# The token halves of a sorted expert stage: copied in a row, and gathered with weights eight columns apart

## The reference, cut to what matters

```python
    g_logits = (t @ w_rg).astype(F32) + b_rg.astype(F32)
    ...
    top_v, top_i = lax.top_k(e_sel, TOP_K_IN_GROUP)
    ...
    hg = jnp.einsum('td,edf->tef', t, w_gate)
    hu = jnp.einsum('td,edf->tef', t, w_up)
    act = jax.nn.silu(hg) * hu * combine[..., None].astype(t.dtype)
    return jnp.einsum('tef,efd->td', act, w_down).reshape(b, L, d)
```

## Time and profile before

| | |
|---|---|
| median of 3 runs | 938.12 us (934.38 to 943.42) |
| the profiled execution | 942.36 us, span 940.6 us |
| mean granted TensorE clock | 0.959 of full speed |
| busy: TensorE products / weight loads | 864.2 us / 521.8 us |
| busy: VectorE / ScalarE / GpSimd | 407.9 / 219.3 / 131.4 us |
| moved by DMA | 190.38 MB |

### The profile page before, as it was taken

How to read it: one execution, slowest core, us unless ns; L and a number is a source line. 1 busy time by engine, 2 the same in 40 slices (tenths; PEclk the granted TensorE clock), 3 DMA queues, 4 the chain that set the end, 5 groups by cost and what they waited for, 6 DMA issues and landing times.

```text
span 940.6 us, 12273 instructions
## 1 busy us (share of the span) xinstructions
PE 864.2 (92%) x4528; PEld 521.8 (55%) x4528; DVE 407.9 (43%) x975; ACT 219.3 (23%) x432; POOL 131.4 (14%) x243
## 2 busy tenths in 40 slices
PE   6699999999789969999989999789999999999795
PEld 3377666766557545657446766553444444433473
DVE  3306665457376262433312421714354453444543
ACT  0211444323232233223232012420110110100233
POOL 4002059999100000000000030000000000000000
PEclk9799999999889979999999999899999999999797
DMA  9323322323961435686675200099997989999401
GB/s 267 93 90 110 108 81 89 112 90 93 293 196 45 135 112 178 218 283 217 224 260 200 68 1 1 0 395 367 418 419 314 419 358 419 421 370 419 157 0 56
DMA packets 79695, 190.38 MB, mean 202 GB/s; under 512 B 9001, under 2 KB 33897, under 8 KB 67335
## 3 DMA queue, kind: packets, MB, share of 16 engines
q1 hardware_dynamic: 74448, 184.40, 52.9%
q0 software_dynamic: 1600, 4.34, 1.6%
q10 hardware_dynamic: 3583, 0.80, 0.5%
HBM read 184.23 MB, written 5.64 MB: 202 GB/s over the span
## 4 chain that ended last, share of the span: by engine, by line
PE 67%; POOL 11%; DVE 7%; DMA 3%; ACT 3%; SPq 3%; ACTq 3%; issue 2%; DVEq 0%; POOLq 0%
PE bank L2191 12%; PE bank L1848 9%; POOL ring L609 7%; PE bank L1675 7%; PE bank L2211 6%; PE bank L2017 6%; PE bank L2261 4%; PE bank L2057 4%; PE bank L2155 3%; POOL proj L612 3%; PE bank L1961 3%; PE bank L1913 2%; PE bank L1931 2%; DMA gate_w<-in_w_in 1%; SPq L379 1%
## 5 line engine op out<-in xcount | busy, mean ns | idle before, releaser
L1675 PE MATMUL bank<-scratch,ring 128*128 128x320 f32 x512 | 144.5, 439 | 0.0
L2191 PE MATMUL bank<-weights,h_exp 128*64 128x512 f32 (+1 forms) x864 | 127.1, 492 | 2.8 <-DMA weights<-in_w_expert_up 2.8
L1848 PE MATMUL bank<-scratch,gate_w 128*128 128x320 f32 x384 | 117.0, 461 | 9.1 <-DMA gate_w<-in_w_in 8.3
L1675 PEld LDWEIGHTS bank<-scratch,ring 128*128 128x128 f32 x512 | 96.4, 192 | 43.2 <-issue 5.8
L1848 PEld LDWEIGHTS bank<-scratch,gate_w 128*128 128x128 f32 x384 | 76.4, 204 | 43.3 <-DMA gate_w<-in_w_in 9.5
L1526 DVE TENSOR_TENSOR x<-x,bank 128x320 f32<-128x320 f32 x160 | 67.2, 483 | 53.3 <-PE bank L2155 53.3
L2191 PEld LDWEIGHTS bank<-weights,h_exp 128*64 128x64 f32 (+1 forms) x864 | 39.7, 121 | 67.0 <-issue 58.3
L609 POOL TENSOR_SCALAR ring<-scratch,par_w 128x64 f32<-128x64 f32 x120 | 68.8, 600 | 3.0
L2211 PE MATMUL bank<-weights,act_ft 128*64 128x512 f32 (+1 forms) x432 | 61.0, 486 | 0.4 <-DVE act_ft L1543 0.4
L1136 DVE SCALAR_TENSOR_TENSOR proj<-scratch,par_w,proj 128x256 f32<-128x256 f32 x120 | 53.5, 511 | 0.2
L633 POOL MEMSET h_hi<- 64x1024 f32 x1 | 0.9, 946 | 302.5 <-DVE proj L1404 302.5
(11 more groups left out here) (362 smaller groups left out, 1125.9 us busy)
## 6 DMA issues: line engine op xcount, KB each, us to landing
weights<-in_w_expert_gate SPq DMA_DIRECT2D x32, 1024.0 KB, 10.2
weights<-in_w_expert_up SPq DMA_DIRECT2D x32, 1024.0 KB, 12.3
weights<-in_w_expert_down SPq DMA_DIRECT2D x16, 2048.0 KB, 15.2
ring<-in_w_in SPq DMA_DIRECT2D x8, 2048.0 KB, 7.8
ring<-in_cache_k SPq DMA_DIRECT2D x64, 256.0 KB, 4.0
ring<-in_cache_v SPq DMA_DIRECT2D x64, 256.0 KB, 4.1
gate_w<-in_w_in SPq DMA_DIRECT2D x24, 512.0 KB, 6.5
ring<-in_w_branch SPq DMA_DIRECT2D x3, 2048.0 KB, 9.0
```

Of the source, the lines that this page charges most:

```text
L1675: m = MM(bank[b_][:, 0:T], slot(j, DC, GROUP)[:, k, (n % 4) * P:(n % 4 + 1) * P], h[:, k, :], start=k == 0, stop=k == DC - 1)
L1848: m = MM(bank[b_][:, c0:c0 + T], g_w[GW_AT[g]][:, k, :], h[:, k, :], start=k == 0, stop=k == DC - 1)
L2191: m = MM(bank[0][per * p:per * (p + 1), 0:2 * DE // g], h_exp[i % 2][:, k, first_place(n):first_place(n) + per], w_gu[u][:, :, k, columns( ...
```

## The change

The halves are written to `h_hi` and `h_lo` in the order in which they lie in the bank, so that feature `8 p + k` is at place `8 p + k`. The gather's product for chunk c then takes the places c, c + 8, c + 16, ... as its weights, which are the same 128 features as before. Lines after the first hunk are one lower in the changed kernel.

```diff
         def chunked(hs, n_, n):
 
-
-            return hs[0:n, n_ // 2, :].rearrange("t (k p) -> t p k", k=DC)[:, 64 * (n_ % 2):64 * (n_ % 2) + 64, :]
+            return hs[0:n, n_ // 2, 512 * (n_ % 2):512 * (n_ % 2) + 512]
...
-                src, scale = h_bank[n_][0:n, :].rearrange("t (p k) -> t p k", k=DC), token_scale[0:n, b:b + 1]
+                src, scale = h_bank[n_][0:n, :], token_scale[0:n, b:b + 1]
                 F(chunked(h_hi, n_, n), src, ACT.Copy, scale=scale).then_inc(s("h_hi_ready"), 1)
...
-                STT(chunked(h_lo, n_, n), h_bank[n_][0:n, :].rearrange("t (p k) -> t p k", k=DC), token_scale[0:n, b:b + 1],
+                STT(chunked(h_lo, n_, n), h_bank[n_][0:n, :], token_scale[0:n, b:b + 1],
                     chunked(h_hi, n_, n).bitcast(F32), ALU.mult, ALU.subtract).then_inc(s("h_lo_ready"), 1)
...
-                    f, ni = slice(c * P, (c + 1) * P), turn_places(i)
+                    f, ni = slice(c, D, DC), turn_places(i)
                     for b in range(3):
                         MM(gather_bank(i, c)[:, 0:ni], h_hi[:, b, f], pick_t[:, b, 0:ni], start=b == 0, stop=False)
```

## The result

| | before | changed |
|---|---|---|
| median of 4 runs | 938.37 us (934.38 to 943.42) | 959.56 us (955.51 to 964.12) |
| ratio | | 1.0231, 95% interval 1.0191 to 1.0271 |
| profiled execution | 942.36 us, span 940.6 | 955.51 us, span 953.6 |

It is slower clear of noise; whether by 2% is open, since the interval begins at 1.0191.

The account below looks back on a forecast made before the run. TensorE was taken to bound the sorted-expert stretch from 625.1 to 870 us. 13.1 us in turns 1 to 3 plus 1.8 net in turn 0 gave 14.9, so 953 us for the median, range 934 to 961.

Parts of the forecast that it names:

- Copies: Copies into `h_hi` and `h_lo`: contiguous writes shorten the chain before the gather by 0.8 us together.
- The load's price: Gather's weight loads on TensorE: the step adds 110 ns, a load every 220 ns; chance 0.46 for 190 to 250 ns.
- 60 ns per doubling: Upper bound for the gather's weight loads, from transposing loads: 60 ns for each doubling of the step, making 180 ns.
- The 144 products: Gather products of turns 1 to 3, in the TensorE-bound stretch: together 13.1 us longer.
- The 9 chunks after `home`: Gather chunks right ahead of the down products, whole on the chain: 9 x 0.62 = 5.6 us longer.
- the 10 under the pause: Chunks in items of two groups, while `act_s` is made: 0.18 us of cover each, 10 x 0.44 = 4.4 us.
- The 5 in items of four groups: Chunks whose transpose follows the gather at 0.85 us: no cover, 5 x 0.62 = 3.1 us longer.
- The 48 products: Turn 0's gather products beside the weights' flight: 4.2 us longer, 1.8 us net with the 0.8 us gain included.
- the clock for the input tiles: Products of tiles 5 to 7: a lower granted clock falling elsewhere moves their time by up to 1.4 us either way.
- No price: Rival for the gather's loads: the step costs nothing, leaving only the 0.8 us gain, 937.3 us; chance 0.33.
- Partial price: Rival for the gather's loads: the step costs 60 ns, a load each 170 ns, 5.3 us more, 943.4; chance 0.13.
- The larger price: Rival for the gather's loads: the step costs 180 ns, a load each 290 ns, 966.5 us; chance 0.08.

Follow-up runs that it names:

- the repeat: The changed kernel timed once more on the same chip as its two parts: 956.41 us, ratio 1.0229 to the kernel before.
- the step alone: Kernel before with only the gather's weights taken at every eighth column, copies writing as before: 960.22 us against 938.21, ratio 1.0241.
- turn 0 alone: Kernel before with weights of step 8 only in the 48 gather products of turn 0: 943.20 us against 938.55, ratio 1.0049.
- the ladders: Changed kernel with weight steps 1 to 8 by chunk and copies writing with steps 2, 4, 8, 16, 64 and 1; run once, 951.81 us.
- copies alone: Changed kernel with the gather's weights put back to 128 neighbouring columns, copies still written in a row: 937.14 us against 938.21, ratio 0.9995.
- rows by k: Changed kernel with neighbouring gather weights again and experts' gate and up rows loaded as 128 c + p: 939.17 us against 938.15, ratio 1.0003.
- turns 1 to 3 alone: Kernel before with weights of step 8 only in the 144 gather products of turns 1 to 3: 958.31 us against 938.55, ratio 1.0209.
- step 2: Kernel before with every second column as weights in all gather products: 938.06 us against 938.15, ratio 0.9999.
- bank read apart: Kernel before with only the copies' loop order changed, reading the bank 32 bytes apart and writing runs of 64: 937.34 us against 938.15, ratio 0.9991.
- the last experiment: Kernel before with step 8 weights only in the gather products after the first turn: 958.31 us against 938.55, ratio 1.0209.

## Why the prediction was right, and where it was not

Sign, place and mechanism were right, and the measured median lies in the range (934 to 961), near its upper end; that range was so wide that it held a change of nothing as well. 953 was 6.6 us too low. Of these the account of the profiled executions finds 3.6: 0.8 in turns 1 to 3 (13.9 for 13.1) and 2.8 before the first silu (4.6 for 1.8). The other 3 are scatter between executions: against the repeat, 956.4, the forecast is 3.4 too low.

**Copies.** Right: forecast 0.8 us, measured 0.73 on the chain. The part given to ScalarE's third copy (0.1 us) is zero: 10.71 us from the token sums to the first `h_lo` copy in both kernels.

**The load's price** is the term that was mis-sized. I took 110 ns more, a load each 220 ns; it is 242 in turn 0 and 230 to 242 elsewhere. ScalarE's copy was the right kind of row, for its price too has reached its end at 16 bytes, but each engine has its own figure for it (0.86 and 0.64 ns an element for the copies, 0.96 a column for the load, from 107 to 230 ns), and that ScalarE's came so near was luck. The transposing load was the wrong kind: it pays at step 2, where the gather's loads pay nothing, and "60 ns per doubling", my upper bound, is no law. By my own formula 242 ns give 16.2 us for turns 1 to 3 and 2.9 for turn 0, 19.1 in place of 14.9. But 16.2 is 2.3 more than was measured there: the price was too low and the cover too, and the two errors partly cancel.

**The 144 products.** Forecast 13.1, measured 13.9 in an execution without a fall of the clock. The 9 chunks after `home` cost 0.75 us each, the 10 under the pause 0.42 (from 1.48 to 1.90 us between gate/up products and `home`): they had 0.33 us of cover, not the 0.18 that the start of the transposes showed, since the two transposes now take 0.25 us of the chain instead of 0.51. The 5 in items of four groups cost 0.65, some 0.1 less than the full length. 6.8 + 4.2 + 3.2 = 14.2.

**The 48 products.** Forecast 4.2 us longer and 1.8 net of cover and gain. Measured 5.3 longer and 4.6 net. Beside the larger load (1.1) it is the clock (1.7): the gather no longer ended early, TensorE waited 1.18 us for VectorE's `home` work with the weights already there, and then ran the first half at 1.2 GHz. I had bounded the clock for the input tiles (up to 1.4 us) and nowhere else.

That the slow gather brings this fall about is not shown. All five profiles with slow loads in turn 0 have it (the changed kernel twice, the step alone, turn 0 alone, the ladders), but so have three of the six with neighbouring weights or step 2 there: copies alone, rows by k, turns 1 to 3 alone. In rows by k the first half takes the same 5.35 us, and the second half still waits 0.16 us for its weights:

```profile
612.85 5.35 PE L2190 MATMUL bank<-weights,h_exp 128*64 128x512 f32 x16 [2.03 <-DMA weights<-in_w_expert_up]
618.37 3.65 PE L2190 MATMUL bank<-weights,h_exp 128*64 128x512 f32 x16 [0.16 <-DMA weights<-in_w_expert_up]
```

So with a quick gather such a fall hides for the most part in the wait for the second half (1.2 us where there is no fall), and what the later gather does for certain is to take that wait away: the fall then costs its full 1.7 us. From the token sums to the first silu the six take 38.0 to 40.6 us, the changed kernel 44.8 and, in the repeat, where tiles 5 to 7 ran at full clock, 42.3.

**The clock in the items' stretch** was missing from the forecast. Between first and last silu the kernels without the step in turns 1 to 3 all take 245.6 us (or 245.7: before, copies alone, step 2, bank read apart, rows by k, turn 0 alone; no granted clock under 0.97 in any microsecond). The four profiled with it take 259.5, 261.2, 261.2 and 262.6, with 0, 1, 1 and 2 falls; each costs 1.5 to 1.7 us. The two kernels that were run once fit: one fall in this stretch with the ladder of weights, six with 64 moved columns and float32r steps up to 7. The changed kernel's wide runs fit too: the mean granted clock of its two short executions (955.5 and 955.9) was 0.965, of the two long ones (963.2 and 964.1) 0.957 and 0.955. Over 960 us that is, as an estimate, 15 to 19 us more at 1.2 GHz, worth some 8 us if half of such time is lost; where in the execution it lay no trace shows. That the sparser gather brings the falls about is read from twelve profiles and was not tested by itself.

**The rivals.** No price (0.33) fell to the step alone (960.22 us) and the ladder: there is no price up to step 2, and step 8 is far beyond. The reading that carried it, that a step only brings a load to the ordinary rate, holds for the transposing load at best. The TensorE page's figure (TensorE: Matmul & The Clock Gate, section LDWEIGHTS, of the Trainium skill) of columns / 1.2, 107 ns, is what we measured at step 1 (107 with 64 moved columns), and would have gone wrong at step 8 by its silence. Advanced Engine Details and Errata (the Trainium skill, section Memory Cachelines) asks for at least two hits on a 16-byte line; the runs agree for writes and weights alike: 8 bytes free, 16 full price. Partial price (0.13) would have been step 3, 170 to 175 ns. The larger price (0.08, 290 ns) is out: the far-apart load ends at 242.

## What to carry to other kernels

Before a weight operand is taken with a step, put the load's own spacing beside the product's: a float32r load of 128 columns had 107 ns of pace under a product of 107 to 120, so doubling it came out nearly whole on TensorE, 192 times, and only pauses and the weights' flight hid a part. Up to 8 bytes between columns is free under such a product; from 16 bytes on it costs the same up to the 32 bytes tried. When data has to be regrouped, let the side that is free pay: the same copies reading the bank 32 bytes apart and writing in runs had the whole gain.

## What the runs showed of the hardware that I had not expected

- The price is by the share of 16 bytes that is used: 107 to 117 ns (up to 8 bytes), 170 (12), 213 to 242 (16 to 32) for float32r; 28 to 33 (up to 8), 43, 53 and 60 ns for bfloat16 at 12, 14 and 16 bytes. Bfloat16 loads follow each other 3.5 to 4 times as quickly as float32r ones at every spacing.
- ScalarE and VectorE have the same edge in their writes: step 2 733 and 752 ns, step 4 1175 and 1143, step 64 no more (1087, 1067, on 64 rows).
- Reading a bank 32 bytes apart cost ScalarE and VectorE nothing (681 and 732 ns against 682 and 736).
- The granted clock fell to 1.2 GHz in the middle of a stretch in which TensorE counts as busy throughout (5.00 of 5.00 us, 801 to 806 us in the last experiment); within the items' stretch only in kernels whose products waited for slow loads.
- Splitting 8 KB pieces of the weights' transfers into 2 KB ones raised the DMA share from 93.9% to 102.1% for the same bytes, and cost no time.
